# Value product of the prompt's attention: 64 moving columns of one key/value head in place of the 128 of a pair

## What is computed

```python
logits = jnp.einsum('bqhgd,bqjhd->bqhgj', q, k_sel).astype(jnp.float32) * (A_HEAD_DIM ** -0.5)
logits = jnp.where(valid[:, :, None, None, :], logits, -jnp.inf)
p = jax.nn.softmax(logits, axis=-1).astype(v.dtype)
o = jnp.einsum('bqhgj,bqjhd->bqhgd', p, v_sel)
```

## Time and profile before

| | us |
|---|---|
| median of 3 runs (lowest, highest) | 3271.43 (3265.44, 3275.41) |
| span of the profiled execution | 3271.5 |
| PE busy over the span | 3011.8 (92%) |
| PEld busy | 2784.5 (85%) |
| DVE busy | 1614.3 (49%) |
| ACT busy | 929.2 (28%) |
| POOL busy | 706.5 (22%) |
| mean granted TensorE clock | 0.958 of full |

### The profile page before, as it was taken

The page is one execution under the profiler, slowest core; times in us unless marked ns, Lnnn a source line. Parts: engine busy times, 40 slices in busy tenths (PEclk is TensorE's granted clock), DMA queues, the critical chain, the costliest instruction groups (busy, mean ns, idle before and its releaser), DMA issues. The chain is left out here.

```text
span 3271.5 us, 45715 instructions
## 1 busy us (share of the span) xinstructions
PE 3011.8 (92%) x17935; PEld 2784.5 (85%) x17935; DVE 1614.3 (49%) x2638; ACT 929.2 (28%) x1640; POOL 706.5 (22%) x397
## 2 busy tenths in 40 slices
PE   6859959989899999999998999986799999999999
PEld 6649948888799989989987989985698999999997
DVE  3069959997234444444445136543324444434435
ACT  3123235667232212112113034433122121121122
POOL 2012110111122121112112145546121112112111
PEclk9779969999899999999999999998899999999999
DMA  3223152112421011011011332317321111101101
GB/s 126 54 65 89 44 133 51 27 33 53 153 73 52 26 51 51 26 51 45 32 51 53 109 111 91 109 65 262 114 67 59 51 36 41 51 27 50 51 26 71
DMA packets 203515, 223.47 MB, mean 68 GB/s; under 512 B 36002, under 2 KB 179298, under 8 KB 203379
## 3 DMA queue, kind: packets, MB, share of 16 engines
q1 hardware_dynamic: 162978, 157.65, 15.8%
q10 hardware_dynamic: 40400, 63.97, 5.9%
HBM read 171.62 MB, written 49.95 MB: 68 GB/s over the span
## 5 line engine op out<-in xcount | busy, mean ns | idle before, releaser
L734 DVE TENSOR_TENSOR h<-mlp_dn_acc,h 128x512 f32<-128x512 f32 x576 | 397.3, 691 | 339.6 <-PE mlp_dn_acc L704 339.6
L723 DVE TENSOR_TENSOR mlp_sq<-mlp_relu 128x384 f32<-128x384 f32 x192 | 165.8, 863 | 554.8 <-ACT mlp_relu L627 554.8
L689 PE MATMUL mlp_up_acc<-end_xT_hi,end_w_hi 128*128 128x384 f32 x768 | 257.8, 336 | 2.3 <-PEq L68 2.3
L689 PE MATMUL mlp_up_acc<-mid_xT_hi,mid_w_hi 128*128 128x384 f32 x768 | 257.6, 335 | 2.3 <-PEq L68 2.3
L689 PE MATMUL mlp_up_acc<-end_xT_hi,end_w_lo 128*128 128x384 f32 x768 | 257.7, 335 | 0.0
L689 PE MATMUL mlp_up_acc<-end_xT_lo,end_w_hi 128*128 128x384 f32 x768 | 257.6, 335 | 0.0
L689 PE MATMUL mlp_up_acc<-mid_xT_hi,mid_w_lo 128*128 128x384 f32 x768 | 257.4, 335 | 0.0
L689 PE MATMUL mlp_up_acc<-mid_xT_lo,mid_w_hi 128*128 128x384 f32 x768 | 257.4, 335 | 0.0
L627 ACT ACTIVATE mlp_relu<-mlp_up_acc 128x384 f32<-128x384 f32 x192 | 94.5, 492 | 561.7 <-PE mlp_up_acc L689 558.0
L704 PE MATMUL mlp_dn_acc<-mid_w_hi,mlp_hid_hi 128*128 128x512 f32 x576 | 224.6, 390 | 0.0
L704 PE MATMUL mlp_dn_acc<-mid_w_lo,mlp_hid_hi 128*128 128x512 f32 x576 | 224.5, 390 | 0.0
(11 more groups left out here) (269 smaller groups left out, 7430.6 us busy)
## 6 DMA issues: line engine op xcount, KB each, us to landing
mid_w_raw<-in_ffn_w_up ACTq DMA_DIRECT2D x15, 1024.0 KB, 5.3
mid_w_raw<-in_ffn_w_down ACTq DMA_DIRECT2D x15, 1024.0 KB, 5.0
end_w_raw<-in_ffn_w_up ACTq DMA_DIRECT2D x15, 1024.0 KB, 5.3
end_w_raw<-in_ffn_w_down ACTq DMA_DIRECT2D x15, 1024.0 KB, 4.9
mid_w_raw<-in_b_w_in SPq DMA_DIRECT2D x11, 1024.0 KB, 7.0
proj_w_raw<-in_a_w_in SPq DMA_DIRECT2D x9, 1024.0 KB, 6.1
att_q_in<-qT SPq DMA_DIRECT2D x16, 512.0 KB, 7.7
qT<-proj0b_stage SPq DMA_DIRECT2D x24, 192.0 KB, 1.8
```

The lines of the kernel that those rows point to most:

```text
L689: mm = pe.matmul(up_acc[:, u % 3, 0:GW], w_up_s[a][:, k, j * P:(j + 1) * P], x_s[c][:, k, g * GW:(g + 1) * GW], start=(n == 0), stop=(n == ...
L723: dve.tensor_tensor(sq[:, u % 2, :], relu[:, u % 2, :], relu[:, u % 2, :], ALU.mult)\
L734: dve.tensor_tensor(cols, dn_acc[:, v % 3, :], cols, ALU.add).then_inc(added, 1)
```

## The change

In the prompt's tiles each product of line 1228 moves the 64 columns of the item's own key/value head, and writes 64 columns of `pv`, where it moved the 128 columns of the pair and wrote 128. Line 1329 reads the first 64 columns of `pv` for every head, where it took the first or the second half by the head's place in its pair. The number of instructions, the stationary operands, the waits and the order of all queues stay. The tile of the running streams (lines 1219, 1221 and 1327) is not touched.

```diff
-                        pair = n % HEADS // (2 * GH4)
+                        kv = n % HEADS // GH4
                         if n == start_of[PROMPT[0]]:
                             pe.wait_ge(v_loaded, 16)
                         for j in range(t + 1):
-                            mm = pe.matmul(dst, probs_T[:, n % 2, j * P:(j + 1) * P],
-                                           vin[:, j, pair * P:(pair + 1) * P], start=(j == 0), stop=(j == t))
+                            mm = pe.matmul(dst[:, 0:HD], probs_T[:, n % 2, j * P:(j + 1) * P],
+                                           vin[:, j, kv * HD:(kv + 1) * HD], start=(j == 0), stop=(j == t))
...
-                        dve.tensor_tensor(dst, pv[:, g % 2, :, (x % 2) * HD:(x % 2 + 1) * HD], by, ALU.mult)\
+                        dve.tensor_tensor(dst, pv[:, g % 2, :, 0:HD], by, ALU.mult)\
```

## The result

The changed kernel is slower. Its median over 7 runs is 3285.96 us (3281.36 to 3291.18), that of the kernel before, run beside it, 3271.61 us (3265.44 to 3277.41): a ratio of 1.0035 with a 95% interval of 1.0021 to 1.0050, some 12 us by the ratio and 14 by the medians. The profiled execution has a span of 3284.3 us. In the table of the experiments further down, one of the five runs of the kernel with 32 columns (3403 us, the one profiled) and two of the ten of the kernel before with the longer pause (6084 and 7519 us) count in the medians but not in the ratios, which take undisturbed runs alone; where the two long times come from is not known.

A forecast was written before the change was run, and what follows sets the result against it. VectorE's top-k rounds, slightly ahead of TensorE, were taken as the limit in tiles 6 and 3, TensorE in tile 2. Low-clock terms gave 3271.5 + 5.1 + 6.6 + 10.4 + 3.4 = 3297 us, range 3265 to 3330.

The forecast's parts named there:

- the term for tile 3: Tile 3 of the attention phase: TensorE's clock stays low through half of the tile, adding 10.4 us.
- The narrow pass saves nothing, 111 ns stay: Line 1228: the load of 128 stationary columns keeps passes 111 ns apart, so TensorE's queue saves nothing.
- Results 54 ns earlier and line 1329 give nothing: Each product's result is out some 54 ns earlier, worth 0.05 us in the last group; line 1329 stays 32 x 425 ns.
- the sign named for it: Profile after, line 1228 in tile 2: six passes still 0.67 us, pass length down from 275 to about 222 ns.
- The clock falls behind the pauses and comes back later: Attention phase: with the array streaming less, TensorE's pauses pull the clock down more often and it returns later; chance 0.58.
- One low stretch more at each of three changes, 5.1 us: Changes of tile from 7 to 4: one more low-clock stretch at each, 3 x 1.7 = 5.1 us.
- Tile 1 low throughout, 6.6 us: Tile 1: after the pause before it the clock stays low through the whole tile, costing 6.6 us.
- the signs named for the forecast: Granted clock in the profile after: below 0.8 in tile 1 and below 0.9 in tile 3 carries the forecast.
- Tile 0 nothing: Tile 0: 16 items at the low clock take 13.6 us in a window of 14.50, so it costs nothing.
- Tile 2, 3.4 us: Tile 2, the last: two low-clock stretches, costing 3.4 us.
- A low stretch costs up to half of itself: Attention phase: a low-clock stretch of 3.4 us costs up to half of itself, priced at 1.7 us.
- The four terms: Low-clock costs: 5.1 us at the changes from 7 to 4, 6.6 in tile 1, 10.4 in tile 3, 3.4 in tile 2.

## Why the prediction was right and where it was wrong

The side was right, and in the main the mechanism, and the size was not: forecast +26 us (3297), measured +14 by the medians and +12 by the ratio. The measured time is inside the range of 3265 to 3330, but the forecast was about twice too large. The step that failed is the term for tile 3, half of it at the low level for 10.4 us, which measured 0.

- *The narrow pass saves nothing, 111 ns stay.* Right. The item in tile 2 keeps its 1.35 us, and the kernel with half a stationary block shows that the load is what holds it. Small correction: where a turn follows a product, 0.05 us an item are won. The record of a turn's load is 0.14 us long and that of a product's 0.19, which fits, but no run took it apart.
- *Results 54 ns earlier and line 1329 give nothing.* Right, though the sign named for it did not come: the median record stayed at 275 ns where about 222 was expected, for a start is no proof, as the prediction says of the 16-column passes. Line 1329 is 425 ns as before, and VectorE's last wait is 2.1 us after 2.3.
- *The clock falls behind the pauses and comes back later.* Right, and shown from three sides: by columns (128 and 96 no loss, 64 12 us, 32 45 us), by cutting the pauses, and by filling them. That it also falls more often is not shown. The Trainium skill has back-to-back matmuls stay warm ("TensorE: Matmul & The Clock Gate", section "Loop structure matters more than you think"); by that nothing would have changed, and it was wrong here.
- *One low stretch more at each of three changes, 5.1 us.* It was two more, none and two more (10.2, 3.4 and 6.8 us of low clock, where it was 3.4, 3.4 and 0). Tiles 6, 5 and 4 lost 1.5, 0.0 and 2.1, together 3.6: more stretches than forecast, each at 0.9 us and not 1.7.
- *Tile 1 low throughout, 6.6 us.* It was low for 10.2 of its 23.9 us and lost 3.2.
- *Half of tile 3 low, 10.4 us.* The step that failed. I let the low level run on from tile 1 into tile 3. It ended 10.2 us after it began, within tile 1, the clock did not fall at the pause before tile 3, and tile 3 lost nothing; and when a longer pause made it fall there, it was back after 3.4 us. Of the signs named for the forecast, the clock below 0.8 in tile 1 came (0.79), the one below 0.9 in tile 3 did not (1.00). I had reckoned with the mean share of narrow passes in an item, the same in all tiles, and concluded that short items keep the clock down. What decided in tile 1 was what TensorE works off behind the pause: in the rows of before it stood already that 13 passes of the product fill most of the low stretch after tile 6. Behind tile 4 it is 30 narrow passes, behind tile 1 only 12. That this is the reason for tile 3 too is argued; no run put more narrow passes there.
- *Tile 0 nothing.* Wrong, and by a sum that its own rows contradict. It took 4 x 213 ns an item, 13.6 us, and called that free in a window of 14.50. But the logits of tile 0 are two passes of 128 columns that take a block's load each, as the prediction itself reads from the earlier trace rows: five passes an item and not four, by its figures 16 x 5 x 213 ns = 17.0 us. It also left out the three items of tile 3, 24 passes, that TensorE works off in this window. Measured are 0.98 us an item, 15.7 us for 16, and with the rest a tile of 19.1 us, 4.6 longer, with TensorE as the limit.
- *Tile 2, 3.4 us.* It lost 1.2.
- *A low stretch costs up to half of itself.* 41 us more of low clock cost 12.8 us of phase, 0.31 us for each us. The long tiles are set by VectorE, whose busy time stayed (269.6 us before, 270.1 after), and its work covers part.

The four terms sum to 25.5 us against 12.6 measured (3.6 + 3.2 + 0 + 4.6 + 1.2); tile 3 alone is 10.4 of the difference, and the terms that were too large in tiles 1 and 2 (by 5.6 together) are about made up by the 4.6 of tile 0 that the forecast did not have, which is luck.

## What to carry to other kernels

A float32 pass that brings a new stationary block of 128 columns each time cost 111 ns here, the load of that block; moving fewer than 128 columns past it saved nothing, and before such a cut one reads the distance between passes, not their length. Less work in the array can cost time through the clock, though no instruction is added: look at the granted clock behind every pause of TensorE, and at what it works off right after it. The cure may lie in the engine that makes the pause: cutting one 1.89 us copy on ScalarE into four pieces took 3.8 us off the phase, more than anything done to the product, though the times of the whole program don't clearly show it. And when a price is put on the low level, count the passes of the shortest items one by one.

## What the runs showed of the hardware

- Dense work does not guarantee the full clock: with 32-column products PE was busy for all of 69.30 us at a granted clock of 0.50, 312 passes without a gap, in the longest of five runs; with 64 columns, for all of the low stretches from 735.7 us (10.20 of 10.20) and from 793.7 us (20.50 of 20.50).
- Passes with 64 stationary columns start 58 ns apart where 128 gave 111, but going over from full to half blocks and back costs, 0.42 us from the first of three turns to the first product against 0.33, and with six passes an item nothing was won (1.37 us against 1.35).
- Nothing is lost at 96 columns and 12 us at 64: the loss doesn't grow evenly with the columns that are missing.
- Tile 7 begins between 509.7 and 522.1 us in traces of kernels that are the same up to there. This scatter of about 12 us is as large as the loss looked for; the length of the one phase in the trace, the same within 0.1 us in two traces of one kernel, seems to tell kernels apart that the times of ten runs could not. Where it comes from was not looked into.
- Why narrow products of tile 0 itself prolong the low stretch there, and those of tiles 1 and 3 don't, and why it lasted 20.5 us in two traces of the changed kernel and 10.2 in the one with the longer pause before tile 3, was not taken apart further.
